# Gathered rows turned on VectorE in 32x32 blocks instead of on TensorE through PSUM

## What is computed

```python
def moe(x, ...):                      # 520 rows of 1024
    scores = sigmoid(x @ w_router)    # 64 experts in 8 groups
    idx = top 8 of the experts of the best 4 groups, per row
    gates = w_sel / sum(w_sel) * 2.5
    y = swiglu(x, w1_s, w3_s, w2_s) + routed_experts(x, idx, gates, w1_e, w3_e, w2_e)

def run_block(e, toks, g):            # for each expert e, the rows that chose it
    xb = x[toks]
    hb = silu(xb @ w1_e[e]) * (xb @ w3_e[e])     # 1024 -> 256
    return (hb @ w2_e[e]) * g                    # 256 -> 1024, added into the rows
```

## Time and profile before

| | us |
|---|---|
| median of 3 runs (lowest to highest) | 1148.23 (1145.43 to 1149.3) |
| span of the profiled execution, the only time the page gives of it | 1144.5 |
| PE, matmuls busy | 1087.3 (95%) |
| PE, weight loads busy | 718.2 (63%) |
| DVE busy | 495.5 (43%) |
| ACT busy | 288.6 (25%) |
| POOL busy | 243.9 (21%) |
| bytes moved by DMA, mean rate | 319.77 MB, 279 GB/s |

### The profile page before, as it was taken

The page is one execution under the profiler, slowest core; times in us unless marked ns, Lnnn a source line. Parts: engine busy times, 40 slices in busy tenths (PEclk is TensorE's granted clock), DMA queues, the critical chain, the costliest instruction groups (busy, mean ns, idle before and its releaser), DMA issues.

```text
span 1144.5 us, 22216 instructions
## 1 busy us (share of the span) xinstructions
PE 1087.3 (95%) x8721; PEld 718.2 (63%) x8721; DVE 495.5 (43%) x1429; ACT 288.6 (25%) x615; POOL 243.9 (21%) x300
## 2 busy tenths in 40 slices
PE   7999998999997989989999999999999999999996
PEld 6888665877883857847555555555556555565531
DVE  0349999224028444681323333233343333423236
ACT  1112163004033041411223222222222322222220
POOL 3120040000000001031333323333333333343300
PEclk9999999999999999998999999999999999999998
DMA  9630315016034853175999999999999999999696
GB/s 331 271 147 1 147 32 183 2 60 251 3 119 148 323 200 133 56 288 217 394 404 409 412 411 415 408 410 414 410 417 410 403 421 407 409 416 387 256 387 262
DMA packets 67122, 319.77 MB, mean 279 GB/s; under 512 B 11069, under 2 KB 17429, under 8 KB 40397
## 3 DMA queue, kind: packets, MB, share of 16 engines
q1 hardware_dynamic: 51269, 278.60, 61.2%
q0 software_dynamic: 14336, 35.48, 8.2%
q10 hardware_dynamic: 1424, 4.35, 1.0%
HBM read 299.36 MB, written 28.58 MB: 287 GB/s over the span
## 4 chain that ended last, share of the span: by engine, by line
PE 73%; DVE 17%; DMA 5%; ACT 2%; issue 2%; SPq 0%; POOL 0%; DVEq 0%; ACTq 0%; POOLq 0%
PE psum L846 65%; PE psum L861 8%; DVE act_mem L1884 7%; DVE mk_mem L2049 2%; DMA arena<-y_rows 2%; DMA mk_mem<-x_rows,idx_x 2%; DMA arena<-in_w_in_dram 2%; DVE act_mem L2105 0%; ACT act_mem L1649 0%; DVE act_mem L2256 0%; DVE act_mem L1984 0%; ACT act_mem L1658 0%; DVE act_mem L2268 0%; DVE act_mem L1982 0%; DVE act_mem L1952 0%
## 5 line engine op out<-in xcount | busy, mean ns | idle before, releaser
L846 PE MATMUL psum<-arena,act_mem 128*32 128x128 f32 (+6 forms) x5488 | 493.4, 365 | 2.1 <-ACT act_mem L1764 1.1
L846 PEld LDWEIGHTS psum<-arena,act_mem 128*32 128x32 f32 (+4 forms) x5488 | 254.4, 120 | 192.6 <-issue 96.7
L846 PE MATMUL psum<-act_mem,arena 128*128 128x260 f32 (+1 forms) x1472 | 328.7, 386 | 8.9 <-DMA arena<-in_w_o_dram 3.8
L846 PEld LDWEIGHTS psum<-act_mem,arena 128*128 128x128 f32 x1472 | 281.0, 196 | 54.1 <-DMA arena<-in_w_o_dram 4.7
L861 PE MATMUL psum<-ident,act_mem 128*128 128x128 f32 (+6 forms) x488 | 79.3, 291 | 15.6 <-DMA act_mem<-in_x_prompt_dram 4.5
L754 POOL DMA_INDIRECT y_rows<-act_mem,idx_y x35 | 39.2, 1120 | 237.4 <-DVE act_mem L2319 214.4
L2317 DVE COPY act_mem<-psum 64x512 f32<-64x512 f32 x35 | 24.3, 693 | 124.7 <-PE psum L846 124.7
L1884 DVE SCALAR_TENSOR_TENSOR act_mem<-act_mem,wcb 128x511 f32<-128x511 f32 (+29 forms) x120 | 77.8, 730 | 0.1
L861 PEld LDWEIGHTS psum<-ident,act_mem 128*128 128x128 f32 (+6 forms) x488 | 57.3, 169 | 29.1 <-issue 17.5
L846 PEld LDWEIGHTS psum<-act_mem 128*96 128x96 bf16 (+5 forms) x419 | 29.9, 123 | 58.2 <-issue 54.6
L2310 DVE SCALAR_TENSOR_TENSOR act_mem<-act_mem,psum 128x128 f32<-128x128 f32 x35 | 12.2, 348 | 114.3 <-ACT act_mem L1720 114.3
(11 more groups left out here) (291 smaller groups left out, 890.8 us busy)
## 6 DMA issues: line engine op xcount, KB each, us to landing
arena<-in_w_e_dram SPq DMA_DIRECT2D x192, 1024.0 KB, 10.2
arena<-y_rows SPq DMA_DIRECT2D x8, 2048.0 KB, 20.4
arena<-in_w_in_dram SPq DMA_DIRECT2D x16, 512.0 KB, 17.7
arena<-in_cache_mem_k_dram SPq DMA_DIRECT2D x8, 1024.0 KB, 8.6
arena<-in_cache_mem_v_dram SPq DMA_DIRECT2D x8, 1024.0 KB, 11.8
arena<-in_w_v_dram SPq DMA_DIRECT2D x1, 4096.0 KB, 24.4
arena<-in_w_k_dram SPq DMA_DIRECT2D x1, 4096.0 KB, 13.9
arena<-in_w_out_dram SPq DMA_DIRECT2D x1, 4096.0 KB, 14.1
```

Source lines behind the costliest of these rows:

```text
L846: return pe.matmul(out, lhsT, rhs, start=first, stop=last)
```

## The change

All experts but the first no longer have their rows turned on TensorE. VectorE turns them straight from `xg` into `xgT`, 32x32 elements at a time: one instruction takes 32 rows and 256 of their numbers, eight blocks, and reads each block with a step of eight numbers. A light expert takes 8 such instructions, a heavy one 12. `xgT` gets 128 columns for each of the eight parts instead of 112. In VectorE's program the step stands ahead of the multiplication of the current expert. In return VectorE gives up its half of a heavy expert's result copy: ScalarE now makes all six pieces. The waits follow (`m_xt` now counts VectorE's turning, `m_xc` and `m_yv` stay at 1 after the first expert).

```diff
@@ PE @@
-            def b_step(e, k, i):
-                n = k % NB
-                pe.wait_ge(m_g[n % 4], 16 * (NB // 4 * i + (k // 4 + 1)))
...
-                (turn_rows if is_big(e) else turn_all)(n).then_inc(m_xt, 1)
...
             def c_step(e, n, wait_w):
-                pe.wait_ge(m_xc, e + 1)
+                if is_big(e):
+                    pe.wait_ge(m_xc, 1)
+                else:
+                    pe.wait_ge(m_xt, e + 1)
...
@@ POOL @@
             def s_step(e, k, i):
                 gp.wait_ge(m_ya, e + 1)
-                if not is_light(n):
-                    gp.wait_ge(m_yv, len(HEAVY) * i + heavies(k))
+                if is_big(e):
+                    gp.wait_ge(m_yv, 1)
...
@@ ACT @@
-            def xc_part(b, cap):
-                return act.activation(xgT[:, b, :, 0:cap],
-                                      psum[:, 1, :].rearrange("p (k s) -> p k s", k=KC)[:, :, ROWS_AT:ROWS_AT + cap], ACT.Copy)
...
             def yh_most(out):
-                act.activation(out[0:LCAP, 0:512], psum[0:LCAP, 0, 0:512], ACT.Copy)
-                for q in range(2):
+                for h in range(2):
+                    act.activation(out[0:LCAP, 512 * h:512 * h + 512], psum[LCAP * h:LCAP * h + LCAP, 0, 0:512], ACT.Copy)
+                for q in range(4):
                     last = act.activation(out[LCAP:MCAP, 256 * q:256 * q + 256],
                                           psum[MORE * q:MORE * q + MORE, 0, 512:768], ACT.Copy)
...
@@ DVE @@
-            def yh_most(out):
-                dve.tensor_copy(out[0:LCAP, 512:1024], psum[LCAP:2 * LCAP, 0, 0:512])
-                for q in range(2, 4):
-                    last = dve.tensor_copy(out[LCAP:MCAP, 256 * q:256 * q + 256], psum[MORE * q:MORE * q + MORE, 0, 512:768])
...
+            def x_step(e, k, i):
+                n = k % NB
+                dve.wait_ge(m_g[n % 4], 16 * (NB // 4 * i + (k // 4 + 1)))
+                if not is_light(n):
+                    dve.wait_ge(m_gm[n % 4], 16 * halves_out(i, k, 4))
+                if at_least(e, 2):
+                    dve.wait_ge(m_h, e - 1)
+                else:
+                    dve.wait_ge(m_xt, 1)
+                for g in range((LCAP if is_light(n) else MCAP) // 32):
+                    at = ROWS_AT + 32 * g
+                    for q in range(4):
+                        rows_in = xg[n % 4][at:at + 32, 256 * q:256 * q + 256].rearrange("p (i k) -> p k i", k=KC)
+                        last = dve.transpose(xgT[32 * q:32 * q + 32, n % 2, :, 32 * g:32 * g + 32], rows_in)
+                last.then_inc(m_xt, 1)
...
             def step(e, k, i, si):
+                if exists(e + 1):
+                    x_step(e + 1, k + 1, i)
                 c_step(e, k % NB)
```

More of the change, by code:

```diff
@@ L1277, in turn_rows @@
                 return last
[L1279 to L1282, removed]
             def up_few(b, part):
@@ L1327, in up @@
                     for k in range(KC):
-                        last = mm(psum[:, 2, at:at + CAP], wu[:, j // 2, k, j % 2:FE:2], xgT[:, b, k, :],
+                        last = mm(psum[:, 2, at:at + CAP], wu[:, j // 2, k, j % 2:FE:2], xgT[:, b, k, 0:CAP],
                                   k == 0, k == KC - 1)
@@ L1358, in a_step, with first_rows @@
                      first_late_hot if isinstance(e, int) and e == SCATTERED else None).then_inc(m_ip, 1)
-            def b_step(e, k, i):
-                n = k % NB
-                pe.wait_ge(m_g[n % 4], 16 * (NB // 4 * i + (k // 4 + 1)))
[L1363 to L1366, removed]
-                (turn_rows if is_big(e) else turn_all)(n).then_inc(m_xt, 1)
+            def first_rows():
+                pe.wait_ge(m_g[0], 16)
+                pe.wait_ge(m_gm[0], 16)
+                turn_rows(0).then_inc(m_xt, 1)
             def c_step(e, n, wait_w):
-                pe.wait_ge(m_xc, e + 1)
+                if is_big(e):
+                    pe.wait_ge(m_xc, 1)
+                else:
+                    pe.wait_ge(m_xt, e + 1)
                 pe.wait_ge(s_w[n % 4], wait_w)
@@ L1440, in _ @@
             pe.wait_ge(s_rz, 2)
-            pe.wait_ge(m_xc, E)
+            pe.wait_ge(m_xc, 1)
             turn_slots(bank("slots0"), 0, onehot[:, 0], MCAP).then_inc(s_full, 1)
@@ L1452, in _ @@
                 pe.wait_ge(m_ya, E)
-                pe.wait_ge(m_yv, heavies(E - 1))
+                pe.wait_ge(m_yv, 1)
                 wait_out(pe, "slots1")
@@ L2364, in c_step, with y_first @@
                     hd_most(n % 2, n).then_inc(m_hd, 1)
-            def y_step(e, k, i, sc):
+            def x_step(e, k, i):
                 n = k % NB
-                if is_light(n):
-                    return
-                dve.wait_ge(m_y, e + 1)
-                if sc is not None:
-                    dve.wait_ge(m_s[n % 2], sc)
-                    dve.wait_ge(m_sm[n % 2], 16 * halves_out(i, k - 2, 2))
-                (yh(ys[:, n % 2, :], n) if is_big(e) else yh_most(ys[:, n % 2, :])).then_inc(m_yv, 1)
+                dve.wait_ge(m_g[n % 4], 16 * (NB // 4 * i + (k // 4 + 1)))
[11 more added lines that the diff above has]
+                last.then_inc(m_xt, 1)
+            def y_first():
+                dve.wait_ge(m_y, 1)
+                yh(ys[:, 0, :], 0).then_inc(m_yv, 1)
             oh_step(0, 0)
@@ L2398, in _, with step @@
             shared_sum(4)
+            x_step(1, 1, 0)
             c_step(0, 0)
-            def step(e, k, i, sc, si):
+            def step(e, k, i, si):
+                if exists(e + 1):
+                    x_step(e + 1, k + 1, i)
                 c_step(e, k % NB)
-                y_step(e - 1, k - 1, i, sc)
+                if is_big(e - 1):
+                    y_first()
                 if exists(e + 3):
@@ L2412, in _ @@
             for k in range(1, NB + 1):
-                step(k, k, 0, None if k <= 2 else 16 * ((k - 1) // 2), None if k < NB - 3 else 16 * ((k + 3 - NB) // 2 + 1))
+                step(k, k, 0, None if k < NB - 3 else 16 * ((k + 3 - NB) // 2 + 1))
             with dve.Fori(1, LAST) as i:
                 for k in range(1, NB + 1):
-                    step(NB * i + k, k, i, 16 * (NB // 2) * i + 16 * ((k - 1) // 2),
-                         16 * (NB // 2) * i + 16 * ((k + 3 - NB) // 2 + 1))
+                    step(NB * i + k, k, i, 16 * (NB // 2) * i + 16 * ((k + 3 - NB) // 2 + 1))
             for k in range(1, NB):
                 e = NB * LAST + k
-                step(e, k, LAST, 16 * ((e - 1) // 2), 16 * ((e + 3 - NB) // 2 + 1))
-            y_step(E - 1, NB - 1, LAST, 16 * scatters(1))
+                step(e, k, LAST, 16 * ((e + 3 - NB) // 2 + 1))
             dve.wait_ge(s_over, 1)
```

27 lines of the change are left out of this document (9 added, 18 removed).

## The result

The changed kernel takes 1205.68 us in the median of 4 runs (1195.66 to 1212.96), against 1147.34 us (1145.43 to 1149.3) for the kernel before in its own 4 runs. The ratio of the runs is 1.0485, with a 95% interval of 1.0448 to 1.0523 (the two medians alone divide to 1.051): slower by 58 us. The profiled execution of the change has a span of 1210.8 us, 66 more than before, so it is one of the longer ones. The direction of the forecast was right and its size was not: 20 us were forecast.

The account below looks back on a forecast made before the run. TensorE and DMA were nearly full, but a ring through the gathers had half a microsecond to spare per four experts. Growing from 36.0 to 37.7 us, it costs 26 us, less 6 for sooner landings: 1168 us, range 1134 to 1208.

Parts of the forecast that it names:

- TensorE's saving: On TensorE: 8 transposes fewer per expert, 1.07 us, 67 us over 63 experts, not all gain because DMA needs 34.7 us.
- p = 0.60: On VectorE: time in us of one block transpose of 32x256 elements; no change in kernel time at p = 0.46.
- the step's price: On VectorE: reading with a step of eight adds 0.20 us to the 0.425 us of a plain copy.
- 30.5 + 12 p: New heavy-expert ring, us for four experts: 12 block transposes of p us plus everything else; 37.7 at p = 0.60.
- ScalarE's copies: On ScalarE: all six result copies of a heavy expert take 2.67 us, 1.1 us more than VectorE's share of 1.57.
- landing time of 7.3 us: On the DMA engines: median time from a gather's issue until its rows land, one term of the sum.
- the ring: Results copied, scattered, next gather, landing, turning, TensorE's work: 35.4 us before against a period of 36.0; 37.7 after.
- Rival D: VectorE becomes the bound: from p = 0.67 if it never waits; 1226 us at p = 0.8; chance 0.08.
- 14% idle time on TensorE: On TensorE: idle time rises from 1% to some 14%, ahead of the hidden turn, released by VectorE's multiplication.
- Less load gives landings back: On the DMA engines: rate falls from 411 to near 390 GB/s, gathers land 0.4 us sooner per turn, 6 us in all.
- The reason given: In VectorE's queue: turning expert e+1 stands ahead of expert e's multiplication, which then queues behind a late gather.
- The range: Kernel time from 1134 us to 1208 us, the upper end being half-rate reading with p = 0.72.

Follow-up runs that it names:

- The copies' kernel: The kernel before with ScalarE making all six copies of a heavy expert's results, nothing else changed: 1177.26 us, ratio 1.0250.
- the ring cut: The changed kernel with POOL issuing the gather of expert e+3 ahead of the scatter of expert e-1: 1192.67 us, ratio 1.0366.
- the filling: The changed kernel with 16 useless TensorE transposes ahead of a light expert's hidden turn: 1184.50 us; with gathers also issued ahead of scatters: 1173.83 us.
- the other order: The changed kernel with expert e's multiplication ahead of the turning of expert e+1 on VectorE: 1459.94 us, ratio 1.2696.
- the plain read: The changed kernel with each block transpose reading its 256 numbers one behind the other, without the step of eight: 1172.71 us, ratio 1.0203.

## Why the prediction was wrong

- **TensorE's saving** (67 us) and that it can't be had in full: right. The transposes are gone from L861.
- **p = 0.60**: 0.641 measured, and the step's price of 0.20 us was right. By the forecast's own formula, 30.5 + 12 p, the miss is worth 0.5 us of 3.2 for each four experts.
- **ScalarE's copies**, 2.67 us: 2.68 measured. But their 1.1 us were in a ring that my sum gave 0.6 us of room, and alone they cost 28 us, not 8. The landing time of 7.3 us was a median taken as a constant; it rose to 7.8 with the copies, and the ring's sum with that is 37.0 us. The copies' kernel took 38.0 for four experts (303.8 us for 32); that it follows the late landings is likely, not shown.
- **What sets the period: this is the step that failed.** The forecast had all four experts' time from one ring, landing to landing through the gathers with one turning of 12 p in it, 37.7 us, and that was to cost 26 us. The runs: with the ring cut, 13 of the 58 us come back and 45 stay. And where the chain of waits follows the ring for a turn, it is not longer than the old period. Pieces in order of time:

```profile
712.16 0.65 DVE act_mem L2355
...
717.45 0.33 DVE act_mem L2292
...
727.00 0.30 DVE act_mem L2281
727.34 0.33 PE psum L861
727.67 7.62 PE psum L846 x104
...
735.45 0.70 ACT act_mem L1745
...
738.34 0.96 POOL act_mem L741
739.60 8.54 DMA act_mem<-x_rows,more_x
748.16 0.63 DVE act_mem L2355
```

  From one landing at 712.1 to the next at 748.1 it passes the 8 transposes of a light expert and the 12 of the heavy one behind it, 20 x 0.65 = 13 us, where the forecast had 12 alone. Still it takes 36.0 us for four experts, against 40.9 in the mean. What takes longer is a loop without a gather in it, in which TensorE and VectorE wait for each other:

```profile
961.90 0.47 PE L861 MATMUL psum<-ident,act_mem 128*128 128x128 f32 x1 [2.55 <-DVE act_mem L2281]
962.30 10.36 PE L846 MATMUL psum<-arena,act_mem 128*64 128x256 f32 x104
972.60 0.28 PE L846 MATMUL psum<-act_mem 128*128 128x6 bf16 x5
972.91 0.17 DVE L2273 TENSOR_REDUCE act_mem<-psum 128x2 f32<-128x6 f32 x1 [1.16 <-PE psum L846]
974.17 7.80 DVE L2355 STREAM_TRANSPOSE act_mem<-mk_mem 32x256 f32<-32x256 f32 x12
982.00 0.29 DVE L2281 TENSOR_TENSOR act_mem<-act_mem,psum 128x128 f32<-128x128 f32 x1
982.35 0.48 PE L861 MATMUL psum<-ident,act_mem 128*128 128x128 f32 x1 [2.38 <-DVE act_mem L2281]
```

  Hidden turn of a light expert, heavy up projection with light down projection, find on TensorE; then the indices, the table, 12 transposes and the multiplication on VectorE: 20.45 us for two experts, 18.0 before. Some 6 of the 10.36 us run at half clock (0.50 in the windows of 1 us from 962 to 968). With the filling, and the clock up, the loop takes 17.7. The forecast had its pieces but never closed it.
- **Rival D** (VectorE the bound) had the right engine and a wrong threshold. I put it at p = 0.67 "if VectorE never waits", from busy time alone, 4.6 + 20 p = 17.4 us a pair at p = 0.64. What counts is occupied time, 2 x 8.97 = 17.9 us with the gaps between its instructions; and at 97% to 100% of the period an engine that also waits for others once or twice an expert holds the others up already. VectorE was to count from a threshold on; it counted below it.
- **The clock**: missing. I forecast 14% idle time on TensorE, in the right place (ahead of the hidden turn, released by L2281 and L2294: 70.5 of 450 us, 15.7%), and priced the idle time alone. It took the clock with it, 19 to 21 us by the runs with filling. That is the forecast's second failed step, a term put at nothing.
- **Less load gives landings back**, 6 us: the DMA rate did fall, further than forecast (362 for 390 GB/s), but the median landing only from 7.3 to 7.1 us, half of the 0.4 us given back for each turn.
- **The reason given** for the loss, the multiplication's place in VectorE's queue: the wait is there, but the other order costs 254 us more.
- **The range**: its upper end, 1208, takes in the 1205.68 measured, but by luck. By the ring's sum p = 0.72 gives 39.1 us and 1195; the 13 us for VectorE on top are not worked out.

In sum, of 58 us some 20 are the clock and some 12 the gathers' ring (both taken out: 1173.83). Some 24 stay. VectorE's own 9.0 us an expert leave no room below the old period, and its waits come on top, 26 of 450 us, of which 5.5 are one stop at the jump of its loop. That VectorE's work is behind the rest is argued from these counts and from the plain read, which took 33 us off; no run took these 24 us apart.

## What to carry to other kernels

When work moves to another engine, add up that engine's whole time for one period, its gaps included, and compare it with the period of today: if it comes within a few per cent, it is the new bound, whatever the sum of busy time says. Follow every loop in which two engines wait for each other until it closes, and add it up as well. Price TensorE's new idle time with what it does to the clock behind it. And before moving work about, look for a queue order that makes fresh loads wait for old results: one exchanged pair of lines on POOL gave what the whole change had been unable to give.

## What the runs showed that was not expected

Useless TensorE work made a kernel faster, 1205.68 to 1184.50 us, by keeping the granted clock at 0.97 for 0.91.

A block transpose of 32x256 float32 costs 0.436 us, as much as a copy of that size (0.425), and 0.641 with a step of eight numbers in its read. Eight or twelve of them, 5.1 or 7.7 us, stand against 1.07 us of TensorE for the same rows (and a copy by ScalarE that TensorE did not wait for). The Trainium skill (VectorE: DVE Perf Modes, Rules for kernel authors) gives 128x128 transposes to TensorE and 32x32 blocks to VectorE. For these rows, which are neither, the runs agree with the first.

VectorE's loop jumps back once, ahead of expert 33. In the kernel before no stop is seen there. With the copies on ScalarE the first instruction behind the jump comes 10.94 us after the one ahead of it, though its input was ready 7 us earlier; the row calls it issue. The changed kernel stops at the same place, ahead of a light expert's transposes:

```profile
845.18 0.35 DVE L2311 SCALAR_TENSOR_TENSOR act_mem<-act_mem,psum 128x128 f32<-128x128 f32 x1 [10.94 <-issue]
852.64 5.12 DVE L2355 STREAM_TRANSPOSE act_mem<-mk_mem 32x256 f32<-32x256 f32 x8 [6.17 <-issue]
```

TensorE waits once for 3.8 us in the first of these kernels and for 5.1 in the second, so some 5 of the change's 58 us may lie here, which neither the forecast nor the experiments price. Gathers first do not take it away (5.3 us). The DMA queue q14, marked instruction, moves 4 packets from 834 to 845 in the first kernel and 3 from 846 to 853 in the second, and none from 810 to 860 in the kernel before. So it is probably the loading of the loop's code; no run tests that.
